# Twenty seven-product pairs with accumulating weight transfers in place of fifteen without

## The reference

```python
def sq_relu_mlp(h, w1, w2):
    return jnp.square(jax.nn.relu(h @ w1)) @ w2      # [256, 8192] @ [8192, 2048]
...
x = x + g2 * sq_relu_mlp(h2, w1[l], w2[l])
return rmsnorm(x, final_norm_g)
```

## Time and profile before

| what | value |
|---|---|
| median of three executions | 1491.27 us |
| the profiled execution | 1491.33 us |
| its span in the trace | 1489.5 us |
| PE busy | 1459.4 us (98%) |
| DVE busy | 1107.0 us (74%) |
| ACT busy | 710.5 us (48%) |
| POOL busy | 115.0 us (8%) |
| granted TensorE clock over the span | 0.998 |

### The profile page before, as it was taken

The page is one execution under the profiler, slowest core; times in us unless marked ns, Lnnn a source line. Parts: engine busy times, 40 slices in busy tenths (PEclk is TensorE's granted clock), DMA queues, the critical chain, the costliest instruction groups (busy, mean ns, idle before and its releaser), DMA issues.

```text
span 1489.5 us, 18858 instructions
## 1 busy us (share of the span) xinstructions
PE 1459.4 (98%) x7252; PEld 1201.0 (81%) x7252; DVE 1107.0 (74%) x1342; ACT 710.5 (48%) x996; POOL 115.0 (8%) x92
## 2 busy tenths in 40 slices
PE   5999999999999999999999999999999999999997
PEld 2567888888888888888888888888888888888886
DVE  2456866867667678998777568778757999789976
ACT  3423444565554453334454434434444666456654
POOL 0000000101000000010100000000301322002200
PEclk9999999999999999999999999999999999999999
DMA  9997776764666679889665577787575665656552
GB/s 368 379 361 261 261 253 210 225 201 144 233 216 229 224 226 356 322 295 356 242 223 155 163 264 273 262 306 268 191 235 177 202 216 187 195 183 222 194 197 81
DMA packets 123053, 355.95 MB, mean 239 GB/s; under 512 B 10962, under 2 KB 11986, under 8 KB 122322
## 3 DMA queue, kind: packets, MB, share of 16 engines
q1 hardware_dynamic: 121348, 353.17, 69.7%
q10 hardware_dynamic: 1616, 1.57, 0.3%
HBM read 352.60 MB, written 2.10 MB: 238 GB/s over the span
## 4 chain that ended last, share of the span: by engine, by line
PE 88%; DVE 5%; ACT 2%; issue 2%; DMA 2%; ACTq 0%; POOL 0%; POOLq 0%; DVEq 0%
PE bank L1691 20%; PE bank L1693 20%; PE bank L1692 20%; PE bank L1977 14%; PE bank L1980 7%; PE bank L1847 2%; DVE wl L1202 2%; PE bank L1820 1%; DMA raw<-in_w_ada 1%; ACT wh L748 1%; PE bank L1722 1%; PE bank L1810 1%; DVE acc L1233 1%; DMA ident<-in_identity 1%; PE bank L1773 0%
## 5 line engine op out<-in xcount | busy, mean ns | idle before, releaser
L1202 DVE TENSOR_TENSOR wl<-raw,wh 128x1024 fp32r<-128x1024 f32 x425 | 527.5, 1257 | 227.6 <-ACT wh L748 209.2
L748 ACT ACTIVATE wh<-raw 128x1024 fp32r<-128x1024 f32 x328 | 341.5, 1059 | 296.8 <-PE bank L1980 141.5
L1977 PE MATMUL bank<-h2S,wh 128*128 128x512 f32 x896 | 245.2, 395 | 0.8 <-DVE wl L1202 0.7
L1691 PE MATMUL bank<-wh,hT 128*128 128x512 f32 x512 | 206.8, 404 | 0.5 <-DVE wl L1202 0.5
L1693 PE MATMUL bank<-wh,hT 128*128 128x512 f32 x512 | 200.1, 391 | 0.0
L1692 PE MATMUL bank<-wl,hT 128*128 128x512 f32 x512 | 199.7, 390 | 0.0
L1977 PEld LDWEIGHTS bank<-h2S,wh 128*128 128x128 f32 x896 | 153.1, 189 | 21.9 <-DVE wl L1202 0.9
L1024 ACT ACTIVATE wh<-raw 128x1024 fp32r<-128x1024 f32 (+1 forms) x128 | 125.8, 1002 | 70.3 <-PE bank L1693 64.2
L1233 DVE SCALAR_TENSOR_TENSOR acc<-raw,cc,acc 128x1024 f32<-128x1024 f32 x120 | 153.5, 1279 | 0.0
L1691 PE MATMUL bank<-wh,hidS 128*128 128x512 f32 x392 | 152.6, 389 | 0.3 <-DVE wl L1202 0.3
L1980 PEld LDWEIGHTS bank<-h2S,wl 128*128 128x128 f32 x896 | 137.5, 189 | 19.0
(11 more groups left out here) (253 smaller groups left out, 2075.9 us busy)
## 6 DMA issues: line engine op xcount, KB each, us to landing
raw<-in_w SPq DMA_DIRECT2D x256, 512.0 KB, 4.7
raw<-in_w_ada SPq DMA_DIRECT2D x192, 512.0 KB, 6.0
raw<-in_w_in SPq DMA_DIRECT2D x128, 512.0 KB, 4.6
raw<-in_w_attn_o SPq DMA_DIRECT2D x32, 512.0 KB, 6.4
raw<-in_w_out SPq DMA_DIRECT2D x32, 512.0 KB, 5.8
raw<-in_w_fourier SPq DMA_DIRECT2D x16, 512.0 KB, 6.8
xt<-in_x SPq DMA_DIRECT2D x2, 1024.0 KB, 6.4
ct<-in_ctx SPq DMA_DIRECT2D x2, 1024.0 KB, 11.0
```

Of the source, the lines that this page charges most:

```text
L748: nc.scalar.activation(slot, raw[:, s % RAW, :], ACT.Copy).then_inc(wh_done, 1)
L1202: nc.vector.tensor_tensor(lo, raw[:, s % RAW, :], hi.bitcast(F32), ALU.subtract)\
L1691: nc.tensor.matmul(bank[b][:], a_hi, w_hi, start=first, stop=False)
L1977: nc.tensor.matmul(out[:], wh[:, slot, cols_f[f]], h2S[:, block, :, :].rearrange("p v t -> p (v t)"), start=(block == 0), stop=False)
```

## The change

Seven-product pairs are 4, 6, 9, 11, 14, 16, 19, 21, 23 and 25 of the first half and 5, 7, 9, 12, 14, 16, 18, 20, 22 and 24 of the second, 20 in place of 15. Some are now two pairs apart. The first two weight sums are no longer made by DVE. w12 of the tile is loaded twice, into both halves of `tS` (two buffers), and a second transfer on the POOL queue adds w11 to the one and w22 to the other in the DMA engines (`accum_op`). The plain loads come from SP, except for the first seven-product pair, where POOL issues them. SP's stand behind the raw tile two ahead of the pair, and wait until the `tS` buffer is free (`t_lo`). POOL makes the first token sums before the first accumulating transfers; afterwards the transfers of a pair stand ahead of its token sums. DVE keeps two weight sums, both now behind the second `wl` of the plain pair, and they wait for the transfers (`t_acc`). ACT makes `tH` first, then the left `wh`, then `aH`; `tH` waits for PE's last use of it (`t_used`). `combine` works in a tile of its own, `comb`, and starts one pair nearer to the last seven-product pair; `prescaled` stands behind pairs 6, 8, 9 and 11.

```diff
--- before.py
+++ after.py
@@ -221,7 +221,7 @@
 PARTS = [(0, 0, 0), (0, 0, 1), (0, 1, 0), (0, 1, 1), (1, 0, 0), (1, 1, 0), (1, 0, 1), (1, 1, 1)]
 STORES = (0, 2, 4, 5, 1, 7, 6)
 
-SEVEN_AT = ((3, 6, 9, 12, 15, 18, 21, 24), (5, 8, 11, 14, 17, 20, 23))
+SEVEN_AT = ((4, 6, 9, 11, 14, 16, 19, 21, 23, 25), (5, 7, 9, 12, 14, 16, 18, 20, 22, 24))
 SEVENS_TO = (len(SEVEN_AT[0]), len(SEVEN_AT[0]) + len(SEVEN_AT[1]))
 NP = DFF // P // 2
 PAIRS, PLAIN = [], []
@@ -232,9 +232,9 @@
         if _seven is None:
             PLAIN.append(len(PAIRS) - 1)
 SEVENS = [i for i, pair in enumerate(PAIRS) if pair[2] is not None]
-COMBINE_AT = {3: ("first", "second"), 4: (0,), 5: (1,), 6: (2,), 7: (3,)}
+COMBINE_AT = {2: ("first", "second"), 3: (0,), 4: (1,), 5: (2, 3)}
 TAKEN_AT = {2: (0, 1), 3: (2, 3)}
-PRESCALED_AT = {6: 0, 9: 1, 12: 2, 15: 3}
+PRESCALED_AT = {6: 0, 8: 1, 9: 2, 11: 3}
 TAIL = 2 * NP - 2
 XS_KEYS = [(0, 0), (0, 1), (1, 0), (1, 1), (0, 2), (1, 2), (0, 3), (1, 3)]
 H2_READY = {t: [2 + XS_KEYS.index((t, k // 4)) for k in range(KT)] for t in range(TB)}
@@ -370,10 +370,12 @@
-        tF = place("tF", [P, 4, HC], F32, "h")
+        tF = place("tF", [P, 2, HC], F32, "h", 4096)
+        comb = place("comb", [P, 4, HC], F32, "h", 16384)
+        tS = [place("tS0", [P, 2, HC], F32, "h"), place("tS1", [P, 2, HC], F32, "f", 4096)]
@@ -527,6 +529,10 @@
+        t_used = sem("t_used")
+        t_start = sem("t_start")
+        t_first = [sem(f"t_first{j}") for j in range(2)]
+        t_acc = [sem(f"t_acc{j}") for j in range(2)]
@@ -628,6 +634,17 @@
                 col, k = divmod(n, DFF // P)
                 sp.wait_ge(wl_done, W2 + n - RAW + 1)
                 sp.dma_start(raw[:, (S2 + n) % RAW, :], w2[k * P:(k + 1) * P, col * NC:(col + 1) * NC]).then_inc(raw_full[(S2 + n) % RAW], 16)
+                if n % 2 == 0 and n // 2 + 1 in SEVENS[1:]:
+                    i = n // 2 + 1
+                    s = SEVENS.index(i)
+                    c, p = divmod(i, NP)
+                    if s == 1:
+                        sp.wait_ge(hid_ready, 4 + 2 * (N1 - 1))
+                    if s >= 2:
+                        sp.wait_ge(t_lo, 2 * s - 2)
+                        sp.wait_ge(t_sum, s - 1)
+                    for j in range(2):
+                        sp.dma_start(tS[s % 2][:, j, :], w2[2 * p * P:(2 * p + 1) * P, c * NC + HC:(c + 1) * NC]).then_inc(t_first[s % 2], 16)
 
             for i in STORES:
                 n, half, t = PARTS[i]
@@ -695,16 +712,35 @@
             sum_row(6)
             sum_row(7)
 
-            pool.wait_ge(hid_ready, 4 + 2 * (N1 - 1))
-            for i in SEVENS:
-                _, p, s, _ = PAIRS[i]
-                k1, k2 = 2 * p, 2 * p + 1
+            def token_sums(s):
+                k1, k2 = 2 * PAIRS[SEVENS[s]][1], 2 * PAIRS[SEVENS[s]][1] + 1
                 if s:
                     pool.wait_ge(a_lo, 3 * s)
                 then(nc.gpsimd.tensor_tensor(aF[:, 0, :], hid[:, k2, P:T], hid[:, k1, P:T], ALU.subtract))
                 nc.gpsimd.tensor_tensor(aF[:, 2, :], hid[:, k1, 0:P], hid[:, k1, P:T], ALU.subtract)
                 then(nc.gpsimd.tensor_tensor(aF[:, 1, :], aF[:, 0, :], hid[:, k1, 0:P], ALU.add))
                 nc.gpsimd.tensor_tensor(aF[:, 3, :], hid[:, k2, 0:P], aF[:, 1, :], ALU.subtract).then_inc(a_sum, 1)
+
+            def weight_sums(s):
+                c, p, _, _ = PAIRS[SEVENS[s]]
+                row, col = 2 * p * P, c * NC
+                if s == 0:
+                    pool.wait_ge(t_start, 32)
+                else:
+                    pool.wait_ge(t_first[s % 2], 32 * (s // 2 + s % 2))
+                nc.gpsimd.dma_start(tS[s % 2][:, 0, :], w2[row:row + P, col:col + HC], accum_op=ALU.add).then_inc(t_acc[s % 2], 16)
+                nc.gpsimd.dma_start(tS[s % 2][:, 1, :], w2[row + P:row + 2 * P, col + HC:col + NC], accum_op=ALU.add).then_inc(t_acc[s % 2], 16)
+
+            pool.wait_ge(gemm_done, M2)
+            p = SEVENS[0]
+            for j in range(2):
+                nc.gpsimd.dma_start(tS[0][:, j, :], w2[2 * p * P:(2 * p + 1) * P, HC:NC]).then_inc(t_start, 16)
+            pool.wait_ge(hid_ready, 4 + 2 * (N1 - 1))
+            token_sums(0)
+            weight_sums(0)
+            for s in range(1, len(SEVENS)):
+                weight_sums(s)
+                token_sums(s)
 
             for t in range(TB):
                 pool.wait_ge(mean_ready, t + 1)
@@ -1031,6 +1067,13 @@
                 tile_hi(2 * i + 1)
 
             def seven_hi(i, p, s):
+                if s:
+                    act.wait_ge(t_used, s)
+                act.wait_ge(t_acc[s % 2], 32 * (s // 2 + 1))
+                nc.scalar.activation(tH[:, 0:2, :], tS[s % 2][:], ACT.Copy).then_inc(t_hi, 1)
+                act.wait_ge(t_sum, s + 1)
+                nc.scalar.activation(tH[:, 2:4, :], tF[:], ACT.Copy).then_inc(t_hi, 1)
+                tile_hi(2 * i, HC)
                 if s == 0:
                     act.wait_ge(row_done, 4)
                 else:
@@ -1039,16 +1082,12 @@
                 nc.scalar.activation(aH[:, 6, :], hid[:, 2 * p + 1, P:T], ACT.Copy).then_inc(a_hi, 1)
                 act.wait_ge(a_sum, s + 1)
                 nc.scalar.activation(aH[:, 0:4, :], aF[:], ACT.Copy).then_inc(a_hi, 1)
-                for j in range(2):
-                    act.wait_ge(t_sum, 2 * s + j + 1)
-                    nc.scalar.activation(tH[:, 2 * j:2 * j + 2, :], tF[:, 2 * j:2 * j + 2, :], ACT.Copy).then_inc(t_hi, 1)
-                tile_hi(2 * i, HC)
                 tile_hi(2 * i + 1)
 
             def copy_p1(c):
                 act.wait_ge(gemm_done, M2 + 2 * SEVENS[SEVENS_TO[c] - 1] + 2)
                 act.wait_ge(t_lo, 2 * SEVENS_TO[c])
-                nc.scalar.activation(tF[:, 0, :], bank[seven_bank(c, 0)][:], ACT.Copy).then_inc(p1_copied, 1)
+                nc.scalar.activation(comb[:, 0, :], bank[seven_bank(c, 0)][:], ACT.Copy).then_inc(p1_copied, 1)
 
             def last_square(i):
                 n, half, t = PARTS[i]
@@ -1552,31 +1591,27 @@
                 for e in range(2):
                     n = 2 * i + e
                     split_lo(W2 + n + 1, S2 + n, wh[:, n % SPL, :], wl[:, n % SPL, :])
-                    if following is not None:
-                        block_sums(i + 1, following, e)
-
-            def block_sums(i, s, step):
-                n1, n2 = 2 * i, 2 * i + 1
-                r1, r2 = raw[:, (S2 + n1) % RAW, :], raw[:, (S2 + n2) % RAW, :]
-                if step == 0:
-                    dve.wait_ge(raw_full[(S2 + n1) % RAW], 16 * ((S2 + n1) // RAW + 1))
-                    dve.wait_ge(raw_full[(S2 + n2) % RAW], 16 * ((S2 + n2) // RAW + 1))
-                    if s:
-                        dve.wait_ge(t_hi, 2 * s)
-                    nc.vector.tensor_tensor(tF[:, 0, :], r1[:, 0:HC], r1[:, HC:NC], ALU.add)
-                    nc.vector.tensor_tensor(tF[:, 1, :], r1[:, HC:NC], r2[:, HC:NC], ALU.add).then_inc(t_sum, 1)
-                else:
-                    dve.wait_ge(t_sum, 2 * s + 1)
-                    then(nc.vector.tensor_tensor(tF[:, 2, :], tF[:, 0, :], r2[:, HC:NC], ALU.add))
-                    nc.vector.tensor_tensor(tF[:, 3, :], tF[:, 2, :], r2[:, 0:HC], ALU.add).then_inc(t_sum, 1)
+                if following is not None:
+                    block_sums(i + 1, following)
+
+            def block_sums(i, s):
+                n2 = 2 * i + 1
+                r2 = raw[:, (S2 + n2) % RAW, :]
+                dve.wait_ge(raw_full[(S2 + n2) % RAW], 16 * ((S2 + n2) // RAW + 1))
+                dve.wait_ge(t_acc[s % 2], 32 * (s // 2 + 1))
+                if s:
+                    dve.wait_ge(t_lo, 2 * s)
+                then(nc.vector.tensor_tensor(tF[:, 0, :], tS[s % 2][:, 0, :], r2[:, HC:NC], ALU.add))
+                nc.vector.tensor_tensor(tF[:, 1, :], tF[:, 0, :], r2[:, 0:HC], ALU.add).then_inc(t_sum, 1)
 
             def seven_lo(i, p, s):
                 n1, n2 = 2 * i, 2 * i + 1
                 for j in range(2):
                     dve.wait_ge(t_hi, 2 * s + j + 1)
-                    dve.wait_ge(t_sum, 2 * s + j + 1)
+                    if j:
+                        dve.wait_ge(t_sum, s + 1)
                     part = slice(2 * j, 2 * j + 2)
-                    nc.vector.tensor_tensor(tL[:, part, :], tF[:, part, :], tH[:, part, :].bitcast(F32), ALU.subtract).then_inc(t_lo, 1)
+                    nc.vector.tensor_tensor(tL[:, part, :], (tS[s % 2], tF)[j][:], tH[:, part, :].bitcast(F32), ALU.subtract).then_inc(t_lo, 1)
                 dve.wait_ge(a_hi, 3 * s + 2)
                 for part, src in ((slice(4, 6), hid[:, 2 * p:2 * p + 2, 0:P]), (slice(6, 7), hid[:, 2 * p + 1:2 * p + 2, P:T])):
                     nc.vector.tensor_tensor(aL[:, part, :], src, aH[:, part, :].bitcast(F32), ALU.subtract).then_inc(a_lo, 1)
@@ -1590,17 +1625,17 @@
             def combine(c, step):
                 if step == "first":
                     dve.wait_ge(p1_copied, c + 1)
```

(14 more changed lines are left out.)

## The result

| | before | after |
|---|---|---|
| median | 1491.20 us (6 runs) | 1496.37 us (6 runs, 1495.13 to 1498.47) |
| profiled execution | 1491.33 us | 1495.13 us |
| span | 1489.5 us | 1493.3 us |

The changed kernel takes 1.0033 of the time of before, 95% interval 1.0020 to 1.0046: slower by 0.33%. The forecast was 1489.1 us, 2.2 us less than the profiled run before and within what it called no change. The measured time is 7.3 us above it, inside the stated range of 1487.6 to 1499 but on the other side of the kernel before.

What follows compares the result with a forecast made beforehand. The prediction took PE to bound the last stage, with DVE almost as full. From 1491.33 us it took 3.40 for matmuls and 0.2 for a wait, and added 1.4 of second-half stalls: 1489.1 us, range 1487.6 to 1499.

Steps and rivals of the forecast that it cites:

- What bounds the kernel: Last stage, hid times w2: PE sets the end, busy 30.00 of 30 us, with DVE almost as full behind it.
- the price of a product: Last stage on PE: a block product is three matmuls, 0.680 us; five more seven-product pairs save 3.40 us.
- DVE's account: Last stage: a plain plus a seven-product pair (distance of two) costs DVE 10.51 us against PE's 10.20.
- The second half: Second column half: DVE's lead runs out at pairs 9, 20, 22 and 24; PE stalls 1.4 us in all.
- lead account: DVE's lead over PE at each seven-product pair, carried pair by pair; it gave no stall in the first half.
- rival C: Descriptor writing for accumulating transfers holds DVE 0.54 us per seven-product pair: 1494.2 us, chance 0.20.
- POOL's start: First half, pair 4: token sums start at 1145.6 and take 4.5 us, so accumulating transfers go out at 1150.1.
- Landing: Pair 4's accumulating transfers land in 5 to 8 us; DVE wants them about 1154, with nearly 3 us lead: zero cost.
- Rival D: Accumulating transfers land late, after 11.6 us, so DVE stands at the block sums: about 1502 us at 15 us, chance 0.14.
- The 11.6 us of the steady stretch: Transfers' allowance: out at T + 4, wanted by DVE at T + 15.6; T is the lead point two pairs before.
- Load: DMA traffic of two pairs: 308 GB/s, or 360 with accumulating bytes counted twice, against 385 moved earlier; no cost.
- SP: Two added 256 KB loads per seven-product pair delay queued raw loads by one pair of four buffered: zero cost.

Runs made afterwards that it cites:

- e5: Changed kernel with the first start loads on SP, 21 seven-product pairs (11 in the first half, from pair 5), prescale steps moved late in the second half: 1487.61 us.
- e2: Changed kernel with the two plain loads of the first tS issued by SP behind raw tile 9, not by POOL: 1492.08 us.
- e7: Kernel before with two plain 256 KB loads that nobody reads put on POOL ahead of its first token sum: 1495.19 us.
- e10: Changed kernel with the second transfers into tS made plain, overwriting instead of adding, so the output isn't the reference's: 1489.98 us.
- e1: Changed kernel with the first half's first pairs moved later (6, 8, 10, 12 for 4, 6, 9, 11), still 20 pairs: 1488.58 us.
- e9: e4 with the changed kernel's ACT order (tH first, waiting for t_used), its earlier combine, and the omitted gate step restored: 1506.50 us.
- e6: e1 with the four prescale steps moved behind pairs 25, 27, 28 and 30 of the second half: 1488.19 us.
- e8: Changed kernel with a 128x1 memset into scratch on POOL between the start loads and the wait for hid: 1496.61 us.
- e3: Changed kernel with the first accumulating transfers put ahead of the first token sums on POOL: 1492.58 us.
- e4: Kernel before with the changed kernel's twenty pairs and prescaled places, all four weight sums on DVE, one gate step left out: 1514.65 us.

## Why the prediction was wrong, point by point

- **What bounds the kernel, and the price of a product (0.680 us): right.** From 1180 us on PE is busy 29.78 to 30.00 of each 30 us; e5 gets 3.7 of 4.08 us.
- **DVE's account (10.51 us per distance of two): right.** In the changed kernel two left `wl` in a row begin 10.50 us apart:

```profile
1418.96 2.08 DVE L1622 TENSOR_TENSOR wl<-raw,wh 128x512 fp32r<-128x512 f32 x2
...
1429.46 2.08 DVE L1622 TENSOR_TENSOR wl<-raw,wh 128x512 fp32r<-128x512 f32 x2
```

- **The second half: right in sum and place.** 1.4 us of stands were forecast, 1.1 came: 0.46, 0.15, 0.27 and 0.25 at pairs 9, 20, 22 and 24 in place of 0.6, 0.19, 0.31 and 0.31. In the first half no stand but the one at the start. The prediction had named a stall of the first half as the sign that its lead account was wrong; this one came from the landing of the operands, not from DVE's pace.
- **Nothing for writing descriptors (rival C): right.** DVE's distance of 10.50 us holds four token sums and the issues of two transfers, and is what was worked out with no price for the issues.
- **POOL's start: the step that failed.** "For pair 4 of the first half they go out at 1145.6 + 4.5 = 1150.1". I took the start of the token sum from a trace in which POOL had issued no transfer, and gave POOL's new issues no price. The sum began at 1150.8 and the transfers went out at 1152.7 and 1153.5. e2 and e7 show that the issues cause it. It is 3.2 of PE's 5.5 us (e2).
- **Landing: the term that was too small, and wrongly put at nothing.** "I take 5 to 8, zero cost": 5.2 us for the first, 8.8 for the one that counts. The operands came at 1162.3, where 1154 was wanted and 3 us of lead were there: 8.3 - 3 is the 5.3 us of PE's wait. By the prediction's own figures 1150.1 + 8 = 1158.1 was already past 1154 + 3, so "zero cost" did not follow from 5 to 8. e2, with the transfers out at 1150.35 and 1151.24, prices this term at 2.3 us of stand.
- **The clock: left out.** A stand of 5.5 us cost 1.6 us more in slow matmuls. The prediction counted stands, not what follows them. No lower clock stood in its rows.
- **Rival D (late transfers) had the right mechanism in the wrong place.** I priced it in the steady stretch, and no stand came of it there. At the first pair the allowance was some 7 us, and there I counted 5 to 8 as zero.
- **The 11.6 us of the steady stretch: right in cost, too large as a margin.** DVE does want the transfers at T + 15.5, but where pairs are two apart the transfers mostly go out up to 2 us later than T + 4, since the plain loads land as late as T + 5. The second then takes 6.3 to 9.8 us to land. From pair 9 of the second half on, at distances of two, it came 0.8 to 2.7 us before DVE wanted it, and once, at pair 16, 0.1 us: issued at 1385.63, landed 7.4 us later at 1393.05, wanted at 1393.13. Ahead of that one a token sum on POOL had lasted 5.45 us:

```profile
1376.96 5.45 POOL L719 TENSOR_TENSOR aF<-hid 128x128 f32<-128x128 f32 x1 [4.57 <-DVE aL L1619]
...
1385.63 1.19 POOL L732 DMA_DIRECT2D tS<-in_w  x1
```

- **Load: the byte count was the wrong measure.** 308 GB/s were set against 385 moved. From 1390 to 1420 us the changed kernel moves 316 GB/s at a DMA share of 1.04, the share that went with 385 GB/s in the first 70 us. So there was little room left, if any, and the 360 GB/s, with each adding byte counted twice, was nearer to it than the 308.
- **SP: right in cost.** Raw loads took 6.9 us at the median in place of 4.7, and still made nobody wait, in e5 neither.

With the 7.1 us of pair 4 the sum is 1489.1 + 7.1 = 1496.2 us, against 1496.37. That it meets the median is in part luck. Left out of it are the earlier start of the stage (0.6 us), the stands of before, which were 0.6 and not 0.2, and those of the second half, 1.1 and not 1.4; with them it is 1494.9. The trace read here is that of the run of 1495.13 us, the fastest of the six; why the others take a microsecond more isn't shown.

The Trainium skill (Collectives: The Full Stack, The bandwidth ceiling, on why ReduceScatter is half of AllGather) says that an add in the DMA is dear by its second source read and not by the adding itself, and that it takes two read descriptors per chunk in place of one. e10 agrees in direction: without the add the DMA share is lower by about a tenth, the landing 1.1 to 1.6 us shorter, and the packets half as many. That POOL's share of the issue also falls, 0.88 to 0.55 us, fits fewer descriptors to write; no run separates that.

The Trainium skill (SBUF — State Buffer, SBUF: two separate sides, on the shared pair) has a token sum and a DVE instruction with two SBUF inputs take turns. The trace agrees from the other side: 0.45 us each while DVE stands (1150.81), 0.85 to 1.33 beside it.

## What to carry to other kernels

Where a pipeline is moved to another queue, work out its first turn by itself: the steady turns had 11 us, and the transfers came in time, if barely; the first had some 7, and it alone turned a gain of 2.6 us (e1) into a loss of 5. When a duration is taken as a range, carry its upper end through the sum before calling the cost zero. An engine that has done one kind of work, in the trace that you read, tells nothing of how it starts when another kind is put ahead of it; bound that start by the widest idle gap that you can't explain. And write out leads pair by pair: it gave the time of e9 within 1.5 us and pointed to the pair that had to move.

## What the runs showed of the hardware that was not expected

- A `tensor_tensor` on POOL behind POOL's own first transfers begins 7.7 to 8.5 us after they were issued (changed kernel, e1, e6, e7, e8, e10), 10.2 us behind accumulating ones (e3), where a memset begins at once (e8). With the same transfers issued by SP it begins at once (e2, e5). The cause is open.
- With three accumulating transfers of 256 KB issued, POOL holds the fourth for 6.8 to 6.9 us (changed kernel, e2, e8), each time until 0.25 us after the second has landed (in the changed kernel landed at 1162.25, issued at 1162.51); four plain ones go out in 2.4 us (e10), in half as many packets. That POOL's room for descriptors is full would fit; a larger one was not tried.
- After PE stood 5.48, 5.05 (e8), 3.84 and 3.39 (e4), 2.28 (e2), 2.63 (e3) and 2.98 us (e7), some 6 to 14 matmuls ran at about 0.43 us; after 1.27 us (e10) and up to 1.93 us (e9) none did.
- In the second half two of POOL's token sums last 5.45 us and not 0.84 in the changed kernel; DVE runs at its undisturbed pace in the first of them (`hidS` 0.68 us at 1353.15). They don't belong to the transfers: e4 and e9, which have none, show three and two of 6.66 us, and e5 and e6, where the prescale steps are moved, show none. They cost no time, but the one at 1376.96 used up the lead of the transfers of pair 16. The cause is open.
